# RWKV recurrence: off blocks' products in step 9, decays loaded after the tail blocks, row steps shared by GpSimd and VectorE

## What is computed

```python
w = exp(-exp(logw))                 # decay, one per direction
kk = k * k_k / norm(k * k_k)        # removal key
kt = k * (1 + (a[z] - 1) * k_a)     # key
# for every token, in order (z = 0) or in reverse (z = 1):
S = S * w[z] - (S @ kk) (kk * a[z])^T + v kt^T
y = S @ r
out = ((norm(y_f + y_b) * ln_g + ln_b + bonus * v) * g) @ w_o
```

## Time and profile before

| | |
|---|---|
| Time, 3 runs | 4414.95, 4422.78, 4424.09 us, median 4422.78 |
| Profiled execution: own time, span | 4419.97 us, 4418.7 us |
| Mean granted TensorE clock | 0.925 of full |
| PE, PEld, DVE busy | 3956.6, 2497.4, 1602.6 us |
| ACT, POOL busy | 1037.3, 1051.3 us |
| The recurrence by pairs | about 3081 to 3840 us of the span |

### The profile page before, as it was taken

The page is one execution under the profiler, slowest core; times in us unless marked ns, Lnnn a source line. Parts: engine busy times, 40 slices in busy tenths (PEclk is TensorE's granted clock), DMA queues, the critical chain, the costliest instruction groups (busy, mean ns, idle before and its releaser), DMA issues.

```text
span 4418.7 us, 76769 instructions
## 1 busy us (share of the span) xinstructions
PE 3956.6 (90%) x32827; PEld 2497.4 (57%) x32827; DVE 1602.6 (36%) x3264; ACT 1037.3 (23%) x2228; POOL 1051.3 (24%) x814
## 2 busy tenths in 40 slices
PE   8999999999999899998799998998676767869999
PEld 7977877877888444564233333444565555433443
DVE  4333232233144221462211113204687777232223
ACT  2032111102201321461222222104333333131111
POOL 4334323333354201210101110114434433010000
PEclk9999999999999999999899998998677777889999
DMA  4244221222222212452799998226101110259999
GB/s 163 79 169 144 78 75 58 96 81 91 96 77 87 80 38 66 142 171 100 259 352 346 359 347 324 93 76 185 46 28 38 46 39 23 93 213 409 408 407 366
DMA packets 277198, 701.26 MB, mean 159 GB/s; under 512 B 27488, under 2 KB 78080, under 8 KB 276608
## 3 DMA queue, kind: packets, MB, share of 16 engines
q1 hardware_dynamic: 250608, 637.58, 39.0%
q0 software_dynamic: 26256, 58.79, 4.9%
HBM read 654.61 MB, written 38.93 MB: 157 GB/s over the span
## 4 chain that ended last, share of the span: by engine, by line
PE 35%; DVE 8%; DMA 5%; ACT 4%; issue 3%; POOL 1%; SPq 0%; DVEq 0%; POOLq 0%; ACTq 0%
PE banks L3397 10%; PE banks L2964 6%; PE banks L3423 4%; DMA ring<-in_moe_w 4%; PE banks L3407 3%; DVE arena L2795 2%; DVE arena L2794 2%; PE banks L3370 2%; PE banks L3431 1%; PE banks L3515 1%; ACT arena L1779 1%; PE banks L3553 1%; PE banks L3506 1%; PE banks L3574 1%; PE banks L3540 1%
## 5 line engine op out<-in xcount | busy, mean ns | idle before, releaser
L2964 PE MATMUL banks<-ring,arena 128*128 128x512 f32 x1248 | 541.9, 594 | 0.4 <-DVE arena L2493 0.4
L3005 PE MATMUL banks<-arena 128*128 128x256 f32 x2256 | 505.9, 380 | 2.5 <-DVE arena L2048 1.9
L3397 PE MATMUL banks<-ring,arena 128*64 128x512 f32 x2048 | 471.5, 600 | 12.5 <-DMA ring<-in_moe_w 7.3
L3005 PEld LDWEIGHTS banks<-arena 128*128 128x128 f32 x2256 | 435.1, 199 | 57.4 <-issue 2.2
L2964 PEld LDWEIGHTS banks<-ring,arena 128*128 128x128 f32 x1248 | 235.8, 191 | 288.6 <-issue 285.8
L3005 PE MATMUL banks<-ring,arena 128*128 128x256 f32 x1584 | 356.3, 383 | 1.6 <-DVE arena L2357 1.6
L3005 PEld LDWEIGHTS banks<-ring,arena 128*128 128x128 f32 x1584 | 314.6, 216 | 35.9 <-DVE arena L2357 2.4
L3397 PEld LDWEIGHTS banks<-ring,arena 128*64 128x64 f32 x2048 | 140.6, 137 | 325.3 <-issue 319.3
L3005 PE MATMUL banks<-arena,ring 128*128 128x256 f32 x1280 | 283.0, 379 | 1.2 <-ACT arena L1631 0.7
L1260 POOL TENSOR_TENSOR arena<-ring 128x1024 f32<-128x1024 f32 x47 | 117.5, 2500 | 637.4 <-PE banks L3005 621.7
L3423 PE MATMUL banks<-ring,arena 128*64 128x512 f32 x1024 | 262.6, 665 | 7.0 <-ACT arena L1800 7.0
(11 more groups left out here) (458 smaller groups left out, 5757.6 us busy)
## 6 DMA issues: line engine op xcount, KB each, us to landing
ring<-in_moe_w SPq DMA_DIRECT2D x768, 512.0 KB, 8.8
ring<-in_w_in SPq DMA_DIRECT2D x21, 2048.0 KB, 7.8
ring<-in_ada_w SPq DMA_DIRECT2D x12, 2048.0 KB, 8.0
ring<-in_ada_w SPq DMA_DIRECT2D x24, 1024.0 KB, 5.3
ring<-in_w_up SPq DMA_DIRECT2D x8, 2048.0 KB, 8.3
ring<-in_w_down SPq DMA_DIRECT2D x8, 2048.0 KB, 7.8
ring<-in_na_w_qkv SPq DMA_DIRECT2D x6, 2048.0 KB, 8.0
ring<-in_w_in SPq DMA_DIRECT2D x8, 1024.0 KB, 6.4
```

Source lines behind the costliest of these rows:

```text
L2964: ins = mm(ps[:, 0:ncol], lhs(k), rhs(k), start=(k == 0 and first), stop=(k == nk - 1))
L3005: ins = mm(ps[:, HW * j:HW * (j + 1)], lhs[:, k, j, :] if len(lhs.shape) == 4 else lhs[:, k, P * j:P * (j + 1)], rhs[:, k, :], start=(star ...
L3397: ins = mm(ps, x_chosen[:, b, k, 0:CAP_L], w[x][:, n * W:(n + 1) * W], start=(k == 0), stop=(k == KD - 1))
```

## The change

- The off blocks' products (TensorE) and their eviction (ScalarE) stand in step 9 behind "sum" 1, in banks 4 and 5, where they stood in step 2 behind the lead blocks, in banks 2 and 3.
- The loads of w0, w1, r, a0 and a1 are issued only when the tail blocks of the next pair are in PSUM (`full(sp, "rw_tail", n)`); k and rows are issued as soon as they may be, as before.
- Row steps 1 to 15 run on GpSimd, in one chain after `weigh_keys`; row steps 16 to 30 stay on VectorE, 16 to 19 in step 7, the rest where they stood. The stage semaphore counts three to a pair.

```diff
--- before.py
+++ after.py
+HALF_STEPS = 16
...
@@ plan_recurrence, beside
             if goes_on:
                 plan.add("dve", "rw_lead", n, width=2, bank=4)
-                plan.add("act", "rw_off", n, width=2, bank=2)
...
-        elif i == 9 and follows:
-            side(n + 1, "sum", 1, 6)
+        elif i == 9:
+            if follows:
+                side(n + 1, "sum", 1, 6)
+            if goes_on:
+                plan.add("act", "rw_off", n, width=2, bank=4)
...
@@ SyncE, load_beside
                 load_pair("k", m)
-                sp.wait_ge(sem("rw_scaled"), rw_scaled(n, "B", 0))
-                load_pair("w0", m)
-                sp.wait_ge(sem("rw_scaled"), rw_scaled(n, "B", 1))
-                load_pair("w1", m)
                 sp.wait_ge(sem("rw_bonus_weighed"), n + 1)
                 load_pair("rows", m)
+                full(sp, "rw_tail", n)
+                sp.wait_ge(sem("rw_scaled"), rw_scaled(n, "B", 1))
+                load_pair("w0", m)
+                load_pair("w1", m)
                 load_pair("r", m)
                 sp.wait_ge(sem("rw_scaled"), rw_scaled(n, "T", 0))
                 load_pair("a0", m)
...
@@ GpSimd
+        def invert_blocks(p):
+
+            pool.wait_ge(sem("rw_blocks_stage"), 3 * p + 1)
+            for j in range(1, HALF_STEPS):
+                shape = [P, j, SUB - 1 - j]
+                rest = Y[:, 0:j, j + 1:SUB]
+                kept = arena[:, kept_at:kept_at + j * (SUB - 1 - j)].rearrange("p (c r) -> p c r", c=j)
+                link(G.tensor_tensor(kept, Y[:, j:j + 1, j + 1:SUB].to_broadcast(shape), Y[:, 0:j, j:j + 1].to_broadcast(shape), ALU.mult))
+                ins = G.tensor_tensor(rest, rest, kept, ALU.subtract)
+                if j + 1 < HALF_STEPS:
+                    link(ins)
+            ins.then_inc(sem("rw_blocks_stage"), 1)
...
                 weigh_keys(m)
+            if n < RW_PAIRS:
+                invert_blocks(n)
+            if m < RW_PAIRS:
                 scale_keys(m)
...
@@ ScalarE, beside
-                if goes_on:
-                    off_blocks(n)
...
-            elif i == 9 and follows:
-                side(n + 1, "sum", 1)
+            elif i == 9:
+                if follows:
+                    side(n + 1, "sum", 1)
+                if goes_on:
+                    off_blocks(n)
...
@@ VectorE
-            if lo == 1:
-                dve.wait_ge(sem("rw_blocks_stage"), 2 * p + 1)
+            if lo == HALF_STEPS:
+                dve.wait_ge(sem("rw_blocks_stage"), 3 * p + 2)
...
                 sum_bonus(n)
-                invert_blocks(n, 1, 7)
...
-                    invert_blocks(n, 7, 12)
...
-                invert_blocks(n, 12, 15)
...
-                invert_blocks(n, 15, 20)
+                invert_blocks(n, HALF_STEPS, 20)
                 mask_rb(n, 2)
...
@@ TensorE, beside
                     blocks_of(n, "rw_lead", True)
-                    blocks_of(n, "rw_off", True)
...
-            elif i == 9 and follows:
-                side(n + 1, "sum", 1)
+            elif i == 9:
+                if follows:
+                    side(n + 1, "sum", 1)
+                if goes_on:
+                    blocks_of(n, "rw_off", True)
```

More of the change, by code:

```diff
@@ L1425, in weigh_keys @@
             if p >= 1:
-                pool.wait_ge(sem("rw_blocks_stage"), 2 * p - 1)
+                pool.wait_ge(sem("rw_blocks_stage"), 3 * p - 2)
             G.tensor_tensor(kk, RW_IN["k"], across(rw_rows[:, 0, :], NT), ALU.mult).then_inc(sem("rw_keys_weighed"), 1)
@@ L1883, in inverse @@
             ps = four_banks(full(act, "rw_inv", p, g), CH)
-            act.wait_ge(sem("rw_blocks_stage"), 2 * p + 2)
+            act.wait_ge(sem("rw_blocks_stage"), 3 * p + 3)
             tiles = inverse_of(p, g).rearrange("p (h j) s -> p h j s", j=RW_TILES)
@@ L3579, in join @@
             ps = four_banks(open_("rw_x", p, g), SUB)
-            pe.wait_ge(sem("rw_blocks_stage"), 2 * p + 2)
+            pe.wait_ge(sem("rw_blocks_stage"), 3 * p + 3)
             taken(pe, "rw_off", p)
```

## The result

| | before | after |
|---|---|---|
| Median of the runs timed side by side | 4419.7 us (4) | 4391.27 us (4) |
| Ratio, 95% interval | | 0.9935 [0.9919, 0.9951] |
| Profiled execution: own time, span | 4419.97, 4418.7 us | 4394.11, 4392.8 us |
| Mean granted TensorE clock | 0.925 | 0.929 |

The change takes 28 us off, where 40 were forecast (4383). The changed kernel was timed again beside the last experiments (`d0_after`): 4388.09 us, ratio 0.9924 [0.991, 0.9938], 33 us off.

What follows compares the result with a forecast made beforehand. TensorE and VectorE take turns, so each part was read separately. Pairs 1 to 6 at -6.0 us (-36), pair 7 -3.0, pair 0 -1.3: together -40, from 4420.0 to 4380, or 4383 as runs' median; range 4350 to 4420.

Steps and rivals of the forecast that it cites:

- six periods: The time from pair 1's first transpose to pair 7's; the forecast took 33.1 us off it.
- Part D: Lead, off and tail blocks on TensorE: 5.5 us saved per pair in pairs 1 to 6, bounds 1.3 and 7.6.
- Off blocks in step 9: TensorE, between sum 1 and step 10's u product: 1.4 us added per pair, bounds 0.5 and 2.6.
- The thirty: GpSimd's chained instructions for row steps 1 to 15: 16.6 us in all, bounds 14.1 and 35.
- the heavy rival: GpSimd's short instructions cost more than any row shows and VectorE waits in step 7: 4474 us, chance 0.17.
- signs of being wrong: GpSimd's chain over 21.6 us; 3 us issue gaps in steps 4 to 6; part D near 12; VectorE's instructions longer.
- part A: First 20 us after a pair's first transpose, scan steps 4 to 7, up to row step 16; called VectorE-bound.
- Row step 16: VectorE's first remaining row step, in step 7: start at +18.4 instead of +20.3 us, 1.9 us gained per pair.
- Pair 0, "18.4 against 18.2, nothing": First pair's stretch up to row step 16: 18.4 us with GpSimd's chain against 18.2 before, so no gain.
- the stalls move with the loads: Rival: the moved 1.8 MB stall TensorE in steps 4 to 6, step 7 reached only at +22: 4406 us, chance 0.12.
- the loads do nothing: Rival: part D gains only the off half with its gap, 2.6 us: 4400 us, chance 0.10.
- the 4408 us by the Trainium skill's rule: Whole-change time if instruction fetch is mostly hidden and part D gains only the off products' own time.

Runs made afterwards that it cites:

- a1: The kernel before with only the new load order (w0, w1, r, a0, a1 behind the tail): 4408.56 us, ratio 0.9965.
- a2: The kernel before with only the off blocks moved from step 2 to step 9: 4401.0 us, ratio 0.9952.
- c1: The changed kernel with four more unread 384 KB copies per pair beside the lead and tail blocks: 4403.92 us, ratio 0.9955.
- c2: The changed kernel with loads of k, rows and r cut to two columns from pair 1 on, so computing from other data: 4380.76 us, ratio 0.9905.
- c4_double: The changed kernel with off blocks ahead of sum 1 in step 9 and each of their matmuls issued twice: 4401.99 us, ratio 0.9953.
- a3_rows: The kernel before with only the row steps divided between GpSimd and VectorE: 4424.8 us, ratio 1.0008.
- a4: The kernel before with the new load order and the off blocks' move, all row steps on VectorE: 4395.07 us, ratio 0.9933.
- b1_swap: The changed kernel with the off blocks ahead of sum 1 in step 9: 4390.22 us, ratio 0.9923.
- b2_pair0: The changed kernel with GpSimd's row steps ahead of weighing the next keys, in pair 0 alone: 4390.92 us, ratio 0.9925.

## Why the prediction was right, and where it was not

The sign and the main mechanism held, and the size in the main: 28 us measured (4419.7 to 4391.3), 33 the second time, of 40 forecast. By the pieces of the span; the measured columns are the two profiled executions of the kernel after:

```
                              forecast   measured   again
start of pair 0's inversion     -1.3       -3.7      -4.1
pair 0 to pair 1                -5.5       +5.4      +4.2
six periods                    -33.1      -27.0     -32.2
rest                            -0.4       -0.6      -1.3
sum                            -40.3      -25.9     -33.4
```

*Part D, "I take 5.5".* Right in size: 13.40 to 8.29 us, 5.1 a pair, and 3.3 in pair 7 (2.6 forecast; 1.7 the second time). The forecast's bounds were built on "what sets the last apart is the DMA share", and that is only part of it. a1 and a2 each gained, c1 brought 1.9 us back with a share near 0.5, but c2 kept 1.7 us of gaps with a share of 0.01. Burst and load act together: with 288 records, gaps are 5.90 us beside loads and 3.10 without; with 192, they are 3.32 and 2.35, and 1.72 with next to nothing loading. The Trainium skill ("Runtime: NRT & Kernel Launch", Instruction fetch mechanics) calls the crossing of a block "mostly hidden"; the 1.38 us on issue of c4_double, with next to no DMA ahead of it, disagree. That TensorE waits there for its instructions, which the prediction called not proven, is so: each gap ends a fixed time after a packet, as shown under c4_double. "Behind the next pair's inputs" is one part of the cause; the other is that short matmuls use up their packets faster than they come.

*Off blocks in step 9, "I take 1.4".* In pair 3 VectorE's wait went from 1.26 to 2.61 us. The end of the inversion moves less: 1.0 us from a3_rows to the kernel after, 0.6 from a1 to a4. In a2 it is 1.1 us, but more than half of that is pair 2 alone; the other five give 0.6. So 1.4 was somewhat high. b1_swap took most of it away without moving the time.

*The thirty, "I take 16.6".* 17.26 us. The line through 512 and 768 elements gives 0.23 us for 30 elements and 0.61 for 240; the trace has 0.24 to 0.28 and 0.62 to 0.70. So neither the flat upper bound of 35 us nor a price per run of elements exists here, and the heavy rival (GpSimd too slow) fell, in pairs 1 to 7. The estimate by the page on GpSimd ("GPSIMD Engine Reference", Elementwise — side-by-side cycle accounting, of the Trainium skill), 13 us and the dispatch, would need 4 us of dispatch; no run splits that off, and the rows' 1.77 ns per element are under the 2.6 cycles at 1.2 GHz (2.17 ns) of the Trainium skill. Of the prediction's signs of being wrong one came true without harm: VectorE's state products in part A take 2.54 us a pair in place of 2.18, where VectorE now has time to spare (busy 9.6 to 10.0 of the first 19 us).

*Row step 16, "1.9 us gained".* 1.2 us in pairs 1 to 6; the thirty's 17.26 us for 16.6 are the difference. But the time did not follow: a3_rows is 1.0008 and a4, without the divided rows, can't be told from the whole change. In a3 the six periods stay at 517.3 us (517.7 before), so 1.2 us earlier in each pair's inversion bought nothing there either; after against a4 it bought 5 to 10 us of 495, and pair 0 took 6 to 8 back. Where a3's 1.2 us a pair went is not shown.

*Pair 0, "18.4 against 18.2, nothing".* This is the step that failed: forecast nothing, measured +8.5 us at the end of pair 0's inversion, and 11 of the 14 us by which the sum missed (10 us the second time, more than the 7 by which the whole missed). "GpSimd first weighs the next keys, until +1.7" was read in pair 3 and carried to pair 0. There GpSimd first has its own work until +4.2, and then the keys' weighing waits for the rows' load. GpSimd around pair 0's first transpose (which ends at 3114.98), and VectorE's row step 16, after:

```profile
3117.64 1.54 POOL L1473 TENSOR_TENSOR arena<-ring,arena 128x768 f32<-128x768 f32 x1
3124.40 1.54 POOL L1430 TENSOR_TENSOR arena<-ring,arena 128x768 f32<-128x768 f32 x1 [5.22 <-DMA arena<-in_rw_rows]
3125.90 0.24 POOL L1453 TENSOR_TENSOR arena<-arena 128x30 f32<-128x30 f32 x1
```

```profile
3143.11 0.41 DVE L2814 TENSOR_TENSOR arena<-arena 128x240 f32<-128x240 f32 x1 [12.60 <-POOL arena L1454]
```

The wait is 5.22 us, the thirty start at +10.9, and VectorE stands idle for 12.60 us. The same wait stood in the trace of before, where it cost nothing, since VectorE had its row steps to itself:

```profile
3118.62 1.55 POOL L1457 TENSOR_TENSOR arena<-ring,arena 128x768 f32<-128x768 f32 x1
3125.43 1.75 POOL L1427 TENSOR_TENSOR arena<-ring,arena 128x768 f32<-128x768 f32 x1 [5.26 <-DMA arena<-in_rw_rows]
```

That row was there to be read. a3_rows shows the loss without the other parts (pair 0's inversion +5.8 us, pair 0 to pair 1 +6.6), c2_tiny gets 3.4 us of it back by smaller loads, and b2_pair0 shows that reordering GpSimd's list only moves the wait to the keys. Pair 0's row steps left on VectorE, with the later pairs divided, would be the version to try; it was not run.

*The rivals.* That the stalls move with the loads did not happen in the mean: in a1_loads row step 16 stands at +20.27 (+20.28 before). That the loads do nothing is refuted by a1 and c1. Gaps in steps 4 to 7 do appear once records or loads are moved. Before, there is none over 0.7 us; the kernel after has five of 1.1 to 2.0 us over all pairs, beside GpSimd's chain, and row step 16 is no later. Where the row steps are VectorE's own, one mattered: in a2_off TensorE stood 4.43 us in pair 2, VectorE 3.99 us behind it, and row step 16 started at +23.21 (+20.47 before).

```profile
3268.52 0.37 PE L3670 MATMUL banks<-arena,ring 64*64 64x64 f32 x2 [4.43 <-issue]
```

```profile
3270.12 0.48 DVE L2831 SCALAR_TENSOR_TENSOR arena<-banks,arena 128x64 f32<-128x64 f32 x2 [3.99 <-PE banks L3692]
```

*Slips in the sums.* None changes the forecast. The rival of 4406 us leaves out pair 0's 1.3 us (4404 with it), the 4408 us by the Trainium skill's rule come to 4409, and the thirty are added up with 0.08 us between two where the row has 0.09. The chances of the three outcomes that are faster by more add up to 0.83, where 0.77 is given.

## What to carry to other kernels

Bursts of small matmuls are priced by more than their busy time: split a burst, or place half of it where the engine waits anyway, and keep bulk loads from running beside it; both remove gaps of the same kind, so their gains may add to less than their sum (in the traces here; the times don't tell). When work moves to another engine's list, read what that list waits for at every iteration, the first above all: a wait that costs nothing today becomes the start time of whatever is queued behind it. And an engine that gets faster by 1 us in each iteration may buy nothing; the single-part run (here 1.0008) tells that, the stage's own duration doesn't.

## What the runs showed of the hardware

- GpSimd's elementwise cost stays near one line down to 30 elements per partition: 0.24 to 0.28 us for 30, 0.62 to 0.70 for 240 (strided runs of 16 to 29 elements), 1.09 for 512, all within 0.1 us of that line.
- TensorE can stand 0.8 to 1.4 us on issue in a burst of small matmuls with no data transfer running (c4_double, DMA share 0.00 to 0.02; c2_tiny, 0.01). A data share near 0.5 in part D adds 1.6 us of gaps a pair (c1_dose).
- Each of 231 such gaps in 14 traces ends 1.19 to 1.67 us after an instruction packet of 16384 bytes has landed on q8; two of these packets never start less than 3.26 us apart in the recurrence. Beside loads (share over 0.3) the packet starts later, its own transfer is no longer (0.95 us against 1.08).
- Part D often runs at the lower level of the clock (granted 0.50, which is 1.2 GHz; the earlier trace rows have 0.50 to 0.70). For the same records TensorE is busy 5.96 us at 0.50 (c2_tiny, pair 3) and 4.44 at 0.74 (after, pair 7), so part of what sets pair 7 apart is the clock.
